# The second halves of K in IN: three 256-column products, or one of 512 and one of 256 with a copy and two adds

## The reference

```
mod = silu(c) @ w_ada + b_ada                        # six vectors, 12,288 columns
h = modulate(rmsnorm(x), sh1, sc1)                   # 256 x 2048
proj = h @ w_in                                      # 2048 x 3072: xr, gr, xp
xr = causal_dwconv(xr); hr = rg_lru(xr, two gates)   # a recurrence over the tokens
y_lru = hr * gelu(gr)
y_pool = pool_mixer(xp)                              # moving averages over 2, 4, 8, 16 tokens, then a product
x = x + gt1 * (concat(y_lru, y_pool) @ w_out)        # OUT
```

## Time and profile before

| | value |
|---|---|
| median of three executions | 2548.33 us |
| profiled execution | 2548.53 us |
| its span | 2546.4 us |
| PE busy | 2493.2 us (98%) |
| DVE busy | 1824.7 us (72%) |
| ACT busy | 1178.8 us (46%) |
| half slabs 12 to 23 on PE | 143.5 to 248.1 us of the span |

### The profile page before, as it was taken

The page is one execution under the profiler, slowest core; times in us unless marked ns, Lnnn a source line. Parts: engine busy times, 40 slices in busy tenths (PEclk is TensorE's granted clock), DMA queues, the critical chain, the costliest instruction groups (busy, mean ns, idle before and its releaser), DMA issues.

```text
span 2546.4 us, 40706 instructions
## 1 busy us (share of the span) xinstructions
PE 2493.2 (98%) x15020; PEld 2148.9 (84%) x15020; DVE 1824.7 (72%) x2348; ACT 1178.8 (46%) x1440; POOL 17.5 (1%) x52
## 2 busy tenths in 40 slices
PE   5999999999999999999999999999999999999998
PEld 2788888888888888888888888888888888888887
DVE  3468989996555655787685665676788668875886
ACT  2345444544444444554444554445544444444444
POOL 0000000000000000000000000000000000000000
PEclk7999999999999999999999999999999999999999
DMA  9998978687555565565545455565555555555554
GB/s 396 400 360 336 378 264 294 239 325 260 185 193 189 185 207 174 172 209 195 182 166 175 159 181 189 190 190 190 182 187 185 194 178 182 195 198 182 184 171 125
DMA packets 159041, 556.70 MB, mean 219 GB/s; under 512 B 16576, under 2 KB 22720, under 8 KB 158928
## 3 DMA queue, kind: packets, MB, share of 16 engines
q1 hardware_dynamic: 157600, 551.94, 63.0%
q0 software_dynamic: 1328, 3.21, 0.4%
HBM read 552.47 MB, written 2.10 MB: 218 GB/s over the span
## 4 chain that ended last, share of the span: by engine, by line
PE 85%; DVE 9%; issue 2%; ACT 2%; DMA 2%; SPq 0%; DVEq 0%; ACTq 0%
PE ps L607 52%; PE ps L614 25%; DVE split L1297 2%; PE ps L604 2%; DMA ride<-in_w_ada 2%; PE pm L632 1%; DVE acc_ada L1362 1%; PE ps L611 1%; ACT split L949 1%; PE ps L589 1%; PE ps L590 0%; PE ps L591 0%; DVE x_t L1462 0%; DVE val L1317 0%; DVE ssq L1380 0%
## 5 line engine op out<-in xcount | busy, mean ns | idle before, releaser
L1297 DVE TENSOR_TENSOR split<-raw,split 128x1024 fp32r<-128x1024 f32 (+1 forms) x864 | 1030.8, 1203 | 618.6 <-ACT split L949 614.4
L949 ACT ACTIVATE split<-raw 128x1024 fp32r<-128x1024 f32 (+1 forms) x864 | 896.7, 1043 | 1112.9 <-PE ps L614 995.7
L607 PE MATMUL ps<-h_s,split 128*128 128x512 f32 x3688 | 1166.5, 398 | 7.5 <-DVE h_s L1440 3.7
L614 PEld LDWEIGHTS ps<-h_s,split 128*128 128x128 f32 x3688 | 694.8, 188 | 164.5
L607 PE MATMUL ps<-mid_s,split 128*128 128x512 f32 x2336 | 734.9, 396 | 0.7 <-DVE split L1297 0.4
L614 PE MATMUL ps<-h_s,split 128*128 128x256 f32 x3688 | 726.2, 278 | 0.0
L607 PEld LDWEIGHTS ps<-h_s,split 128*128 128x128 f32 x3688 | 564.1, 189 | 15.6 <-issue 9.8
L614 PEld LDWEIGHTS ps<-mid_s,split 128*128 128x128 f32 x2336 | 438.8, 188 | 103.8
L614 PE MATMUL ps<-mid_s,split 128*128 128x256 f32 x2336 | 458.9, 278 | 0.0
L607 PEld LDWEIGHTS ps<-mid_s,split 128*128 128x128 f32 x2336 | 355.7, 189 | 4.2 <-issue 2.7
L956 ACT ACTIVATE low<-ps 128x512 f32<-128x512 f32 x238 | 137.8, 579 | 0.0
(11 more groups left out here) (278 smaller groups left out, 1427.0 us busy)
## 6 DMA issues: line engine op xcount, KB each, us to landing
raw<-in_w_in SPq DMA_DIRECT2D x224, 512.0 KB, 3.7
raw<-in_w_ffn_down SPq DMA_DIRECT2D x128, 512.0 KB, 4.3
ride<-in_w_ada SPq DMA_DIRECT2D x44, 1024.0 KB, 10.2
raw<-in_w_ffn_gate SPq DMA_DIRECT2D x88, 512.0 KB, 3.9
raw<-in_w_ffn_up SPq DMA_DIRECT2D x88, 512.0 KB, 4.2
raw<-in_w_ffn_a SPq DMA_DIRECT2D x88, 512.0 KB, 4.2
raw<-in_w_ffn_b SPq DMA_DIRECT2D x88, 512.0 KB, 4.5
raw<-in_w_out SPq DMA_DIRECT2D x64, 512.0 KB, 4.6
```

Of the source, the lines that this page charges most:

```text
L607: pe.matmul(ps[:, s, b, :], split[:, slot, k, 0, b * P:(b + 1) * P], acts[:, k0 + k, :, :].rearrange("p h t -> p (h t)"), start=start, sto ...
L614: mm = pe.matmul(ps[:, s, b, 0:T], split[:, slot, k, 1, b * P:(b + 1) * P], acts[:, k0 + k, 0, :], start=False, stop=stop)
L949: act.activation(split[:, c, 0:kt, 0, :], raw[:, CHUNKS * s + c, 0:kt, :], ACT.Copy).then_inc(hi_ready, 1)
L1297: dve.tensor_tensor(split[:, c, 0:kt, 1, :], raw[:, CHUNKS * s + c, 0:kt, :], split[:, c, 0:kt, 0, :].bitcast(F32), ALU.subtract).then_inc ...
```

## The change

The 12 half slabs 12 to 23 use `multiply` as the others do: per block of 128 rows and half slab two products (512 and 256 columns) in place of three of 256. That is 384 in place of 576 products over the 24 chunks. At the end of each of the 12 half slabs ACT gets a `copy_low`, and DVE's single add becomes two: left half of PSUM plus `low`, then that plus the partial sum. The functions `multiply_narrow` and `evacuate_narrow` go.

```diff
-        def multiply_narrow(G, slot, s, acts, k0, kt, first, last, ready=None):
...
-                    pe.matmul(ps[:, s, b, 0:T], weights[:, 0, :], x[:, 0, :], start=start, stop=False)
-                    pe.matmul(ps[:, s, b, 0:T], weights[:, 0, :], x[:, 1, :], start=False, stop=False)
-                    mm = pe.matmul(ps[:, s, b, 0:T], weights[:, 1, :], x[:, 0, :], start=False, stop=stop)
-            mm.then_inc(chunk_used, 1)
...
-                form = multiply if E < HALF_SLABS else multiply_narrow
-                form(2 * E + c, (2 * E + c) % RING, E % 2, h_s, k0, KT, c == 0, c == 1,
-                     ready=k0 if E % HALF_SLABS == 0 else None)
+                multiply(2 * E + c, (2 * E + c) % RING, E % 2, h_s, k0, KT, c == 0, c == 1,
+                         ready=k0 if E % HALF_SLABS == 0 else None)
...
-            if E < HALF_SLABS:
-                copy_low(E, E % 2, 2 * E + 2)
+            copy_low(E, E % 2, 2 * E + 2)
...
-        def evacuate_narrow(E, s, dst, plus):
-
-            dve.wait_ge(chunk_used, 2 * E + 2)
-            dve.tensor_tensor(dst, ps[:, s, :, 0:T], plus, ALU.add).then_inc(evacuated, 1)
-            dve.wait_ge(evacuated, E + 1)
-            unsplit[0] += 1
...
-            evacuate_narrow(E, E % 2, partial(q) if q < 8 else val[:, q % 2, :, :], partial(q))
+            evacuate(E, E % 2, partial(q) if q < 8 else val[:, q % 2, :, :], plus=partial(q))
```

## The result

The changed kernel takes 2551.96 us (median of 22 runs, 2551.4 to 2552.95) and the kernel before 2548.32 (22 runs beside them): 3.6 us more, ratio 1.0015 with a 95% interval of 1.0009 to 1.0021. The forecast was 2551.4, range 2549.0 to 2553.8. The profiled execution took 2552.49, 3.96 more than that of before. Of all runs named here one is far off and left out of its ratio: one of the eleven with the first six half slabs took 5007.85 us, the other ten 2546.14 to 2548.13. PE is as busy as before in share, and DVE has 8.3 us more to do in 12 more instructions.

What follows compares the result with a forecast made beforehand. From 206 us to the end of OUT DVE's queue was taken to set the time. PE's saving of -1.2 and adds of +4.3 gave +3.1 us, so 2551.6 profiled and 2551.4 us median, range 2549.0 to 2553.8.

Steps and rivals of the forecast that it cites:

- PE's saving counts up to DVE's first convert: Chunks 24 to 36, before DVE's convert at 206.05 us: fewer products save PE 0.094 us per chunk, 1.2 us earlier.
- the 0.3 us that stood beside it as an estimate: Chunks 24 to 36: PE's saving by the Trainium skill's issue gap, 0.02 us per chunk; the sum would be +4.0.
- Adds of half slabs 12 to 17 covered: Up to 206 us DVE's waits hide the added 0.72 us per half slab; at the shortest wait 0.08 us are left.
- Adds of half slabs 18 to 23: From 206 us DVE has no cover, so six added adds of 0.72 us cost 4.3 us.
- Copies and DVE's new wait, nothing: Half slabs 12 to 23: ACT's 12 copies of 0.58 us and DVE's wait for them cost nothing; at most 1.2 us for copies.
- Rival 3: ACT from 242 to 253 us: PE's gain fails and copies are late, 5.5 us slower, 2553.8 us; chance 8%.
- The end chain and OUT carry the delay to the end: From half slab 23's add to OUT's end there is no slack, so OUT's fourth chunk and end come 3.1 us later.
- PE's waits: Waits grow to about 5 us for `pool_low(1)`, above 1 ahead of half slab 23, about 2 at OUT's fourth chunk.
- rival 2: PE's clock falls in the longer wait for `pool_low(1)`, costing up to 1.9 us, 2553.3 us; over 1 us: chance 10%.

Runs made afterwards that it cites:

- experiment 2: The kernel before with only half slabs 18 to 23 in the new form; 2552.70 us, ratio 1.0017.
- experiment 3: The kernel before with the new products in all 24 chunks, but no copy and still one add per half slab; 2546.70 us, ratio 0.9995.
- experiment 1: The kernel before with only half slabs 12 to 17 in the new form; 2546.33 us, ratio 0.9994.
- experiment 4: The kernel before, old products and no copy, with a second DVE operation of the same size after each add of half slabs 12 to 23; 2553.03 us, ratio 1.0019.
- experiment 5: The changed kernel with the fourth pool product moved from behind half slab 21 to behind half slab 22; 2552.24 us, ratio 1.0018.
- experiment 8: The changed kernel with 20 extra PE products of 512 columns ahead of half slab 21's last chunk; 2551.78 us, ratio 1.0016.
- experiment 7: The changed kernel, unaltered, run again for a second profile; 2550.41 us in one run.
- experiment 6: The kernel before with only half slabs 12 to 18 in the new form; 2548.08 us, ratio 1.0003.

## Why the prediction was right, point by point

- *PE's saving counts up to DVE's first convert, 1.2 us.* It came as 1.13 (1.00 to 1.13 in the versions that have it in half slabs 12 to 17); the 0.3 us that stood beside it as an estimate did not hold. Behind that point it bought nothing: experiments 2 and 3.
- *Adds of half slabs 12 to 17 covered, with 0.08 us left at the tightest place.* That wait has just vanished and DVE is not late; experiment 1 puts their cost at nothing.
- *Adds of half slabs 18 to 23, 6 x 0.72 = 4.3 us.* 4.35 in the account, shown by the last six alone (+4.16) and by six bare operations of DVE (+4.40). One reading behind it was off: of the 1.8 us in which DVE was not busy from 206 us on, the two waits of about 0.4 are 0.8, so not most; the rest lies between its other instructions.
- *Copies and DVE's new wait, nothing.* Shown by experiment 4, which has neither, and by 5 and 8, which have both. Rival 3 (2553.8) is out: its late converts came, 0.63 us of them, but from PE.
- *The end chain and OUT carry the delay to the end.* OUT is 87.54 us in both, and the rest equal within 0.1.
- *PE's waits.* About 5 us for `pool_low(1)`: 5.00. About 2 us at OUT's fourth chunk, at 261.9: 1.65, at 262.72. Above 1 us ahead of half slab 23: wrong, there is none, since PE at half its clock came to that place late. With the clock kept up (experiment 8) it waits 1.16 there.
- *The step that was mis-sized: rival 2.* I had the fall of the clock in the long wait as likely and its cost as hidden, up to 1.3 us that PE has to spare. It fell in all four profiles with a wait of 4.4 to 5.0 us. In the changed kernel PE is at 0.50 from 235.24 to 239.6, which loses half of 4.4, 2.2 us, 0.9 more than the 1.3; the converts are late by 0.63 in sum. So the forecast took the mechanism at zero where it costs 0 (experiment 2) to 1.3 us (experiment 7). Its 0.63 in the first profile is about the 0.6 by which the measured 2551.96 lies above 2551.4; that the median holds just this much of it is not shown. Rival 2 gave 10% to a cost over 1 us, and one of the two profiles of the changed kernel has it.

By the Trainium skill (TensorE: Matmul & The Clock Gate, section Why this matters for your kernels) idle gaps between bursts of matmuls put PE back to half rate. The waits of 2.85 to 5.00 us here agree. The shorter ones show that from the length of a wait alone it could not be told: 2.19 and 2.82 us left the clock at 1.00, and 1.75 and 1.78 us were followed by a fall.

Open: what decides that a wait of 1.75 to 1.78 us ahead of OUT is followed by a fall in experiments 5 and 8 (0.53 and 0.55 in the window from 264 to 266, in which the clock also rises again), and one of 1.65 by 1.00 in the changed kernel. In the two where it fell the clock had been up, or had recovered earlier, ahead of it; no run varied that by itself. The version with the first six beats both kernels in the trace (1.0 us less up to OUT than before) and by its median (1.9 less than the 2548.19 of before beside it). Against before the interval of the ratio holds 1, so by time alone its gain is not certain; of the 2.3 us between the two profiled executions 1.4 are a shorter opening stage, which the change does not touch.

## What to carry to other kernels

Work out which engine's queue has no gaps in the stretch of the change, and from where on: an operation added there costs its start-to-start time in full, and what another engine saves counts only ahead of that point. A change of form need not be made everywhere: put it into the part whose waits cover its cost, as the first six half slabs did. And a longer wait of PE is not free even where it looks hidden, because what follows it may run at half its clock; look at what the engines behind it have to spare then.

## What the runs showed of the hardware

- PE's granted clock was at 0.50 behind waits of 2.85 and 3.00 us (experiments 5 and 6), and stayed at 1.00 behind 2.19 and 2.82 (1 and 3). Counted from the end of the wait the low stretch was about 3 us (5: 232.30 to 235.1) to 6 us long (6: 233.18 to 239.1), and for the same wait in the same kernel (5.00 and 4.99) it made converts late by 0.63 and by 1.26 us.
- Giving PE 2.4 us of useless products in place of a 3.0 us wait made the stretch up to OUT 2.29 us shorter in the profile and the median 0.7 us lower, and the runs' spread fell from 4.8 us (2546.35 to 2551.18) to 1.7 (2546.51 to 2548.24).
- Three products of 256 columns in place of one of 512 and one of 256 cost 0.087 us more per chunk of four blocks (1.13 over 13 chunks, read at the start of DVE's first convert).
